# Output projection of a hybrid encoder: blocks begun with the first two head groups, later tiles turned between the halves

## The reference

```python
def hybrid_mixer(h, w_in, ..., g_out_a, g_out_b, g_out_c, w_o):
    ...
    y = jnp.concatenate([rms_norm(flat(out_a), g_out_a),      # 6 heads, columns 0 to 383
                         rms_norm(flat(out_b), g_out_b),      # 6 heads, columns 384 to 767
                         rms_norm(flat(out_c), g_out_c)], axis=-1)   # 4 heads, columns 768 to 1023
    return jnp.einsum('bsf,fd->bsd', y, w_o)

# in the layer:  x = x + hybrid_mixer(...);  h = rms_norm(x, g_ffn);  ...
```

## Time and profile before

| | us |
|---|---|
| median of 3 runs | 2483.45 (2481.55 to 2484.16) |
| the profiled execution | 2487.08 |
| its span, first to last instruction | 2485.4 |
| TensorE busy | 2393.0 (96%) |
| VectorE busy | 739.6 (30%) |
| ScalarE busy | 571.5 (23%) |

### The profile page before, as it was taken

How to read it: one execution, slowest core, us unless ns; L and a number is a source line. 1 busy time by engine, 2 the same in 40 slices (tenths; PEclk the granted TensorE clock), 3 DMA queues, 4 the chain that set the end, 5 groups by cost and what they waited for, 6 DMA issues and landing times.

```text
span 2485.4 us, 40198 instructions
## 1 busy us (share of the span) xinstructions
PE 2393.0 (96%) x16824; PEld 2236.3 (90%) x16825; DVE 739.6 (30%) x1499; ACT 571.5 (23%) x1116; POOL 121.1 (5%) x108
## 2 busy tenths in 40 slices
PE   7999998999999999989989999999989999999998
PEld 7988876788879888779989989999989999999996
DVE  5566742434745566640000000010000010100104
ACT  3355521222433454421010001010010010100102
POOL 1130100000001120010000000000000000000001
PEclk9999999999999999999999999999999999999999
DMA  8210247323220210467766666778867687787883
GB/s 259 94 50 1 83 125 256 119 75 126 110 104 28 85 50 8 150 257 285 288 227 247 234 229 221 293 258 300 302 238 284 238 325 294 284 299 289 326 304 121
DMA packets 204711, 488.68 MB, mean 197 GB/s; under 512 B 5105, under 2 KB 31872, under 8 KB 204144
## 3 DMA queue, kind: packets, MB, share of 16 engines
q1 hardware_dynamic: 193408, 434.60, 47.7%
q0 software_dynamic: 8944, 42.91, 5.5%
q10 hardware_dynamic: 2176, 8.39, 0.8%
HBM read 465.17 MB, written 37.49 MB: 202 GB/s over the span
## 4 chain that ended last, share of the span: by engine, by line
PE 89%; DVE 4%; DMA 3%; issue 2%; ACT 2%; SPq 0%; DVEq 0%; ACTq 0%
PE ps L1084 35%; PE ps L1099 17%; PE ps L983 9%; PE ps L788 5%; PE ps L994 5%; PE ps L934 4%; PE ps L766 3%; DMA weight_ring<-in_w_dram 2%; PE ps L808 1%; PE ps L809 1%; PE ps L811 1%; PE ps L799 1%; PE ps L800 1%; PE ps L801 1%; PE ps L1040 1%
## 5 line engine op out<-in xcount | busy, mean ns | idle before, releaser
L1084 PE MATMUL ps<-hT,attention_arena 128*128 128x132 f32 (+3 forms) x4096 | 528.6, 285 | 22.7 <-issue 21.8
L1084 PEld LDWEIGHTS ps<-hT,attention_arena 128*128 128x128 f32 x4096 | 509.7, 191 | 24.5 <-issue 24.5
L1894 DVE TENSOR_TENSOR attention_arena<-ps,attention_arena 128x256 f32<-128x256 f32 x224 | 95.1, 425 | 1202.9 <-ACT attention_arena L1428 1202.9
L1084 PE MATMUL ps<-hT,weight_ring 128*128 128x132 f32 (+3 forms) x3072 | 395.4, 284 | 0.0
L1084 PEld LDWEIGHTS ps<-hT,weight_ring 128*128 128x128 f32 x3072 | 380.6, 190 | 0.0
L1428 ACT ACTIVATE attention_arena<-ps 128x256 f32<-128x256 f32 x224 | 85.8, 383 | 1131.9 <-PE ps L1084 1131.8
L1099 PE MATMUL ps<-attention_arena 128*128 128x132 f32 (+3 forms) x2048 | 266.7, 283 | 0.0
L1099 PEld LDWEIGHTS ps<-attention_arena 128*128 128x128 f32 x2048 | 254.6, 190 | 0.0
L983 PE MATMUL ps<-x_high,w_parts 128*128 128x512 f32 x704 | 225.8, 402 | 11.6 <-DVE w_parts L1642 10.0
L1099 PE MATMUL ps<-attention_arena,weight_ring 128*128 128x132 f32 (+3 forms) x1536 | 200.0, 283 | 0.0
L1099 PEld LDWEIGHTS ps<-attention_arena,weight_ring 128*128 128x128 f32 x1536 | 190.9, 190 | 0.0
(11 more groups left out here) (268 smaller groups left out, 2615.1 us busy)
## 6 DMA issues: line engine op xcount, KB each, us to landing
attention_arena<-in_e_w_dram SPq DMA_DIRECT2D x96, 2048.0 KB, 12.3
weight_ring<-in_e_w_dram SPq DMA_DIRECT2D x72, 2048.0 KB, 12.2
weight_ring<-in_w_dram SPq DMA_DIRECT2D x22, 1024.0 KB, 7.8
weight_ring<-in_w_dram SPq DMA_DIRECT2D x4, 2816.0 KB, 11.0
weight_ring<-in_w_o_dram SPq DMA_DIRECT2D x4, 2048.0 KB, 7.9
attention_arena<-rows_by_slot POOLq DMA_DIRECT2D x8, 1024.0 KB, 11.6
results_by_slot<-attention_arena ACTq DMA_DIRECT2D x8, 1024.0 KB, 10.2
weight_ring<-in_w_in_dram SPq DMA_DIRECT2D x2, 3072.0 KB, 11.2
```

The source lines that it names most:

```text
L1084: last = nc.tensor.matmul(ps[:, f % 2, m * UNIT:m * UNIT + n], w[:, k, i * P:(i + 1) * P], XT[:, k, 0:n], start=(k == 0), stop=(k == ND - 1))
L1894: tt(eh[:, f % EHS, :], ps[:, f % 2, UNIT:2 * UNIT], esil[:, f % 2, :], ALU.mult).then_inc(gu_free, 1)
```

## The change

On TensorE the first job of tile 0 waits for a new signal, raised by the norm of group B of tile 0, and no longer for the third group. Tile 0's second job still waits for the third group. `out_times` is split: it multiplies the first four depths, then tile t+1 is turned, then the last four depths follow. On VectorE a tile's low parts come ahead of the next tile's three norms instead of behind them. The job table puts each tile's result ahead of the next tile's turned banks. Line numbers in the changed kernel are 1 to 10 higher.

```diff
--- before.py
+++ after.py
@@ -115,9 +115,9 @@
         if p + 1 < len(PAIRS) and g != 1:
             j += prep_at(p + 1, k)
         j.append((("PT", g), "AD"[g % 2]))
-    for t in range(NT + 1):
+    for t in range(NT):
         j += [(("yT", t, i), "D") for i in range(2)] if t < NT else []
-        j += [(("op", t - 1, 0), "D")] if t else []
+        j += [(("op", t, 0), "D")] if t < NT else []
     return j
 
 
@@ -446,6 +446,7 @@
         o_out = sem("head_outputs_stored")
         strip_ready, strip_in, strip_half = sem("strips_ready"), sem("strips_loaded"), sem("strip_half_built")
         y_ready = sem("group_rows_ready")
+        y_first = sem("first_two_groups_of_first_tile_ready")
         gains_free = sem("gains_free")
         dve_link = sem("dve_order")
         out_done = sem("output_stored")
@@ -789,17 +790,18 @@
                                                 start=(k == 0 and v is w_low), stop=(k == kt - 1 and r is rows_high and v is w_high))
                 last.then_inc(filled, 1)
 
-            def out_times(l, t, i):
-
-                b = take(l, "op", t, i)
+            def out_times(l, t, i, ks=range(ND)):
+
+                b = take(l, "op", t, i) if 0 in ks else ps[:, J.bank(l, "op", t, i), :]
                 at = slice(t * P, (t + 1) * P)
-                for k in range(ND):
+                for k in ks:
                     h = o_high[i][k // 2][:, (k % 2) * 512:(k % 2 + 1) * 512]
                     r = out_words(ring_low, l, i, k // 2)[:, (k % 2) * 512:(k % 2 + 1) * 512]
                     nc.tensor.matmul(b, y_high[:, k, at], r, start=(k == 0), stop=False)
                     nc.tensor.matmul(b, y_low[:, k, at], h, start=False, stop=False)
                     last = nc.tensor.matmul(b, y_high[:, k, at], h, start=False, stop=(k == ND - 1))
-                last.then_inc(filled, 1)
+                if ND - 1 in ks:
+                    last.then_inc(filled, 1)
 
             def cols_times(job, w_high, w_low, ks):
 
@@ -953,15 +955,23 @@
                     if g:
                         weigh(g - 1)
                 weigh(STEPS - 1)
-                for t in range(NT + 1):
-                    if t < NT:
-                        pe.wait_ge(y_ready, l * NT + t + 1)
+                def group_rows_turned(t, i):
+                    turn((l, "yT", t, i), [on[:, t, (4 * i + k) * P:(4 * i + k + 1) * P] for k in range(4)])
+
+                pe.wait_ge(y_first, l + 1)
+                group_rows_turned(0, 0)
+                pe.wait_ge(y_ready, l * NT + 1)
+                group_rows_turned(0, 1)
+                pe.wait_ge(out_low, out_part(l, 0, 3))
+                for t in range(NT):
+                    emptied_upto(l, "yT", t, 0)
+                    out_times(l, t, 0, range(0, ND // 2))
+                    if t + 1 < NT:
+                        pe.wait_ge(y_ready, l * NT + t + 2)
                         for i in range(2):
-                            turn((l, "yT", t, i), [on[:, t, (4 * i + k) * P:(4 * i + k + 1) * P] for k in range(4)])
-                    if t:
-                        emptied_upto(l, "yT", t - 1, 1)
-                        pe.wait_ge(out_low, out_part(l, 0, 3))
-                        out_times(l, t - 1, 0)
+                            group_rows_turned(t + 1, i)
+                    emptied_upto(l, "yT", t, 1)
+                    out_times(l, t, 0, range(ND // 2, ND))
                 pe.wait_ge(out_low, out_part(l, 1, 3))
                 if l == LAYERS - 1:
                     pe.wait_ge(router_in, 16)
@@ -1758,7 +1768,7 @@
                         out_low_part(l, 0, OUT_LOW_AT[g])
                 roots_in(0, 2 * NT)
                 group_normed(l, 0, 0)
-                group_normed(l, 1, 0)
+                group_normed(l, 1, 0).then_inc(y_first, 1)
                 head_out(l, NH - 1)
                 dve.wait_ge(o_out, (l + 1) * NH)
                 for t in range(2):
@@ -1766,13 +1776,13 @@
                 dve.sem_inc(sq_done, 1)
                 roots_in(2 * NT, 3 * NT)
                 for t in range(NT + 2):
+                    if 1 <= t <= NT:
+                        turned_low_parts(l, "yT", t - 1)
                     if t < NT:
                         if t:
                             group_normed(l, 0, t)
                             group_normed(l, 1, t)
                         group_normed(l, 2, t).then_inc(y_ready, 1)
-                    if 1 <= t <= NT:
-                        turned_low_parts(l, "yT", t - 1)
                     if t >= 2:
                         out_low_part(l, 1, t - 2)
                         dve.wait_ge(x_back[t - 2], 16 * (l + 1))
```

## The result

| | before | after |
|---|---|---|
| median of 6 runs each, on the same chip | 2484.19 us (2481.55 to 2488.99) | 2493.38 us (2489.32 to 2495.93) |
| ratio to before, 95% interval | 1 | 1.0032 (1.0020 to 1.0043) |
| the profiled execution, its span | 2487.08, 2485.4 | 2489.32, 2487.6 |

The forecast was 2480.6 us, 2.9 under the kernel before. The ratio puts the changed kernel 8 us above it (5 to 11), and the interval excludes no change. The profiled execution of the changed kernel was the shortest of its six runs, so the two spans differ by less than the medians; its head also reached the projection 2.3 us earlier. Hence each stage is compared from its own start: from the end of the last head step (the start and length of the row of 16) to SyncE's load that waits for the last block of the first column half.

The account below looks back on a forecast made before the run. It took TensorE as the bound, with six microseconds per layer between last head step and first block. One layer's clock falling gave about 2.9 us off the 2483.45 median: 2480.6, range 2477.8 to 2484.0.

Parts of the forecast that it names:

- The first turn: Tile 0's first four transposes wait for the second group's norm and run in TensorE's idle time: cost nothing.
- the second turn: Tile 0's other transposes still wait for the third group's norm and start at 296.09, as before.
- the first low part: On VectorE, directly behind the third group's norm: ends at 296.74, so the first block starts at 296.8, 2.2 us sooner.
- The turn of tile 1: Moves from waiting time to between tile 0's halves, on TensorE's path: costs 0.79 us, with no wait or a few hundredths.
- Later tiles: Turned between halves instead of between tiles: no cost, as the added wait for the previous tile's addition has 1.3 us slack.
- slower: the added wait: Rival: VectorE's chain after a turn outgrows 6.4 us, each microsecond over costs 6; up to 2504.0 us; chance 0.04.
- a wait named for the addition ahead of a second half: Sign that would prove the forecast wrong: TensorE waiting there for VectorE to add the previous tile's result to x.
- The gain with the clock up: Start of the output projection at full clock: 2.35 us gained in layer 0, 1.95 in layer 1.
- The clock: A fall to half clock over blocks costs up to 1.5 us a layer; one fall 0.36, two 0.28, none 0.22.
- Other queues: ScalarE unchanged, VectorE's last low part in time, SyncE's dense-weight load moves with the last block and passes the gain on.
- the gain given back in layer 0: Rival: the dense stage's load ending does not move with its start, losing layer 0's gain: about 2482.2 us; chance 0.10.

Follow-up runs that it names:

- e4: The kernel before with nothing changed but the job table, taken from the change: ratio to before 1.0108 (1.0092 to 1.0123), 26.8 us slower.
- e5: The change with the old job table, plus eight spare products between tile 0's two turns: 2481.43 us against 2486.43 before, ratio 0.9979.
- e1: The change with the job table of the kernel before, every engine's queue as in the change: ratio to before 1.0001 (0.9992 to 1.0010).
- e6: The kernel before with twelve spare products per layer in its 2.98 us gap after the last head step: ratio to before 0.9995 (0.9986 to 1.0004).
- e7: The change with the old job table and tile 0's first blocks multiplied ahead of its second turn: ratio to before 0.9985 (0.9977 to 0.9994).
- e2: The change with its new table, but waits for filled banks count in TensorE's real filling order: ratio to before 0.9990 (0.9972 to 1.0008).
- e3: The change with its new table, but emptied banks counted in VectorE's real order: ratio to before 0.9998 (0.9989 to 1.0008).

## Why the prediction was wrong, point by point

- **The first turn, the second turn, the first low part: right.** The first block stands 0.77 us after the second turn's start (said: 0.7), 2.1 us nearer to the last head step than before (said: 2.2).
- **The turn of tile 1 on the path: right.** It takes 0.80 (298.44 to 299.24; said: 0.79), with no wait ahead of it (said: none or a few hundredths).
- **Later tiles, "so no cost": the step that failed.** The prediction saw that the new table changes the counts, but followed only the counts of emptied banks, and those only to the wait ahead of a second half, which is indeed free. It did not ask what else reads the table or compare its order with the order of the fills. `J.filled` reads it too, and the first half waits for a count of emptied banks as well. The term put at 0 measured 1.73 us at each of six seams, 10.4 us.
- **The rival "slower: the added wait" named the wrong end of the chain.** It let VectorE's steps grow past a slack of 1.3 us until the addition came late. VectorE's steps did not grow; their chain began late, at a cast that ScalarE had waited 2.21 us for (302.31). Its sign that something was wrong, "a wait named for the addition ahead of a second half", was not seen in the changed kernel; e4 has such a wait, ahead of whole tiles.
- **The gain with the clock up, 2.35 and 1.95: right within 0.2.** e5 is the change without the wait and without the fall, and its stages are 2.20 and 1.89 us shorter than before.
- **The clock: the chance was badly placed.** The forecast took a fall in one layer (0.36, both 0.28). It fell in both layers in before, after and e1 to e4, and in no layer of e5 and e6, which fill the gap, and of e7, which puts blocks behind it. The sizes were near: with a fall the stages of e1 gain 1.04 and 0.68 (said: 0.85 to 0.9 and 0.45 to 0.7). The rule of the Trainium skill that the prediction weighed (TensorE: Matmul & The Clock Gate, Part 4: PE-mode transpose), that transposes do not bring the array to full clock, fits the fall: four transposes moved into the gap did not keep the clock up, eight products in the same gap (e5) did. It does not fit the rise in layer 1 of the kernel before, which the prediction passed over: only transposes ran from 1021.73 on the earlier trace rows, and the granted clock was back at 1.00 in the stretch from 1024.80 (shown under e6), ahead of the first block. Where the two differ, the measurement decides.
- **Other queues, and the gain given back in layer 0: not settled.** e5's 4.1 us in its stages agree with its time (3.2 to 7.5 less). But at the end of the load that this rival named, at 389.25 in the kernel before, single profiles scatter by more than the gains: counted from the last head step, e5 is 1.6 us ahead of the kernel before there (its stage gained 2.2), e2 2.6 ahead (0.9), e1 0.1 behind (1.0), whose load took 46.86 us instead of 45.20.

With the failed term put in, the sum is 2.9 less 1.2 for the second fall, 1.7 us of gain, against 10.4 of loss: 8.7 us slower, where the ratio gave 8 (5 to 11).

## What to carry to other kernels

A table that gives counts to semaphores is part of the schedule: when a row of it moves, every reader of those counts has to be followed, fills as well as empties, and each has to be compared with the order in which the engines really finish. A wait that the list of waits names for an odd producer (a cast waiting for a product instead of its turn) can be such a miscount. Here it left TensorE idle for 1.47 us at each seam, the part of the late chain that no other work covered. Where TensorE must wait anyway ahead of dense products, products there can be worth trying: with eight spare ones in the gap the clock stayed up and the two stages were 2.4 us shorter than e1's (e5), with real blocks ahead of the second turn 3.3 us (e7).

## What the runs showed of the hardware

Neither the length of the idle time nor what stood behind it accounts by itself for the falls of the granted clock. In after, e1, e2 and e3 four transposes and 2.09 or 2.10 us of idle time, with four more transposes behind, led to a fall in both layers. In e7 four transposes and 2.13 us (1.78 in layer 1) of idle time with blocks right behind them left the clock at 1.00, and in e6 sixteen transposes right behind products did too. But in layer 0 of after the fall came inside the idle time, ahead of the second turn at 293.80, so what ran behind the gap can't have brought it there; in e2 it came at 297.3, a microsecond behind the second turn's start (296.35). And the same wait of 2.33 us in e4 led to no fall behind the one at 309.36 and to one behind the next, at 318.47. So the two layers of e7 are few, and what decides between such cases stays open.

The idle time in layer 0 of after, ahead of its fall and behind it (columns as under e4):

```profile
293.00:293.30 0.30, 0.00 (x0) 1.00 0.92 369
293.40:293.80 0.40, 0.00 (x0) 0.50 0.54 195
```

```profile
294.20:296.90 2.70, 0.63 (x4) 0.39 (x4) 2.03 (x8) 1.80 (x6) 0.00 (x0) 1.00 0.83 328
297.00:300.00 3.00, 3.00 (x15) 2.49 (x16) 2.19 (x5) 0.94 (x2) 0.00 (x0) 1.00 0.00 0
```

These two stretches are e7's (busy time of TensorE, its weight loads, VectorE, ScalarE and GpSimd ahead of the granted clock): the idle time and the blocks behind it, both at 1.00.
